# A two-layer hybrid encoder on one core: gate wait, entry roundings, additions to x, root spread and low halves reordered

## The reference

```python
def _layer(x, pos, l, ...):
    h = _rms(x, attn_norm[l])
    z = h @ w_in[l]                       # dq, dk, dv, c_q, c_kv, k_pe
    dq, dk = _rope(...), _rope(...)       # 4 heads x 2 maps of 64
    y_diff = _diff_attention(dq, dk, dv, lam, diff_subln[l], lam_init)
    qh = _rms(c_q, q_a_norm[l]) @ w_q_b[l]
    kvh = _rms(c_kv, kv_a_norm[l]) @ w_kv_b[l]
    y_mla = _mla_attention(q_nope, q_pe, k_nope, k_pe, v)     # 4 heads
    x = x + concat([y_diff, y_mla]) @ w_o[l]
    h = _rms(x, ffn_norm[l])
    return x + (silu(h @ w_gate[l]) * (h @ w_up[l])) @ w_down[l]   # 2816 wide

y = _rms(_layer(_layer(x, 0), 1), final_norm)
```

## Time and profile before

| | |
|---|---|
| Median of 3 runs | 2415.0 us (2414.55 to 2415.11) |
| The profiled execution | 2414.82 us, of it the span 2413.0 us |
| TensorE busy | 2355.6 us (98%) |
| VectorE busy | 1748.3 us (72%) |
| GpSimd busy | 847.4 us (35%) |
| ScalarE busy | 769.1 us (32%) |
| Mean granted TensorE clock | 0.992 of full speed |

### The profile page before, as it was taken

How to read it: one execution, slowest core, us unless ns; L and a number is a source line. 1 busy time by engine, 2 the same in 40 slices (tenths; PEclk the granted TensorE clock), 3 DMA queues, 4 the chain that set the end, 5 groups by cost and what they waited for, 6 DMA issues and landing times.

```text
span 2413.0 us, 32364 instructions
## 1 busy us (share of the span) xinstructions
PE 2355.6 (98%) x11064; PEld 1950.9 (81%) x11064; DVE 1748.3 (72%) x3031; ACT 769.1 (32%) x1492; POOL 847.4 (35%) x640
## 2 busy tenths in 40 slices
PE   8999999999999999999999999999999999999997
PEld 6877888878888888888788788878788888888875
DVE  7997388777677777766758965898666666666676
ACT  5555145532222222222224532454222222222212
POOL 4313000176666666663200010003544444444422
PEclk9999999999999999999999999999999999999998
DMA  8624541344333333331332235223211111111122
GB/s 302 218 79 147 198 162 53 113 174 134 130 125 127 130 130 120 116 120 59 108 140 106 83 126 208 91 88 131 88 53 52 52 52 52 52 52 52 44 78 79
DMA packets 55105, 266.92 MB, mean 111 GB/s; under 512 B 6496, under 2 KB 6624, under 8 KB 36960
## 3 DMA queue, kind: packets, MB, share of 16 engines
q1 hardware_dynamic: 54288, 264.83, 31.7%
q10 hardware_dynamic: 720, 0.86, 0.1%
HBM read 196.45 MB, written 69.21 MB: 110 GB/s over the span
## 4 chain that ended last, share of the span: by engine, by line
PE 79%; DVE 9%; issue 4%; ACT 2%; POOL 2%; DMA 0%; DVEq 0%; ACTq 0%; POOLq 0%; SPq 0%
PE bank L480 25%; PE bank L482 25%; PE bank L481 24%; PE bank L990 2%; DVE x L1830 2%; PE bank L828 1%; DVE u_lo L1816 1%; DVE silu L1805 1%; POOL w L690 1%; PE bank L836 1%; POOL acc L711 1%; DVE aT_lo L1776 0%; DVE qpe L1651 0%; DMA raw<-in_wffn 0%; POOL w L685 0%
## 5 line engine op out<-in xcount | busy, mean ns | idle before, releaser
L480 PE MATMUL bank<-h_hi,w 128*128 128x512 f32 x1792 | 703.6, 393 | 6.1 <-issue 6.1
L482 PE MATMUL bank<-h_hi,w 128*128 128x512 f32 x1792 | 699.5, 390 | 0.0
L481 PE MATMUL bank<-h_lo,w 128*128 128x512 f32 x1792 | 699.0, 390 | 0.0
L1830 DVE TENSOR_TENSOR x<-x,bank 128x512 f32<-128x512 f32 x768 | 470.7, 682 | 4.2 <-PE bank L482 1.2
L690 POOL TENSOR_TENSOR w<-raw,w 128x512 fp32r<-128x512 f32 x230 | 333.1, 1472 | 268.7 <-ACT w L1364 118.6
L480 PEld LDWEIGHTS bank<-h_hi,w 128*128 128x128 f32 x1792 | 337.6, 188 | 75.7 <-issue 6.9
L482 PEld LDWEIGHTS bank<-h_hi,w 128*128 128x128 f32 x1792 | 337.3, 188 | 71.0
L481 PEld LDWEIGHTS bank<-h_lo,w 128*128 128x128 f32 x1792 | 337.7, 188 | 69.1
L742 POOL TENSOR_TENSOR wd<-down_raw,wd 128x512 fp32r<-128x512 f32 x120 | 162.9, 1366 | 485.0 <-ACT wd L1441 485.0
L480 PE MATMUL bank<-u_hi,wd 128*128 128x512 f32 x560 | 220.9, 394 | 9.8 <-DVE x L1830 4.7
L481 PE MATMUL bank<-u_lo,wd 128*128 128x512 f32 x560 | 218.8, 391 | 0.0
(11 more groups left out here) (213 smaller groups left out, 3967.4 us busy)
## 6 DMA issues: line engine op xcount, KB each, us to landing
w<-parked SPq DMA_DIRECT2D x81, 1024.0 KB, 4.8
raw<-in_wffn SPq DMA_DIRECT2D x88, 512.0 KB, 3.6
parked<-w SPq DMA_DIRECT2D x27, 1024.0 KB, 6.5
parked<-p SPq DMA_DIRECT2D x27, 1024.0 KB, 4.8
down_raw<-in_wffn SPq DMA_DIRECT2D x44, 512.0 KB, 3.6
raw<-in_watt SPq DMA_DIRECT2D x27, 512.0 KB, 4.5
praw<-in_watt SPq DMA_DIRECT2D x27, 512.0 KB, 5.7
x_kept<-x SPq DMA_DIRECT2D x4, 2048.0 KB, 9.4
```

The costliest lines, as they stand in the source:

```text
L480: nc.tensor.matmul(out_ap, lhs[0], rhs[0], start=first, stop=False)
L481: nc.tensor.matmul(out_ap, lhs[0], rhs[1], start=False, stop=False)
L482: return nc.tensor.matmul(out_ap, lhs[1], rhs[0], start=False, stop=last)
L1830: nc.vector.tensor_tensor(xn, xn, bank[banks + m][:], op).then_inc(s_acc.sem, 1)
```

## The change

Six things:
- `TENSOR_ORDER`: `RB y2` goes from behind `P vm1` to behind `P vm2`, in all four halves. (The rest of the table is only wrapped at other places.)
- `GPSIMD_ORDER`: `W 23` goes from between `AD 4` and `AD 5` to behind `AD 7`.
- In the three later halves GpSimd makes the seven low halves of the normed tiles (`later_half`), in the order y0, y1, ckv, cq, cq, y2, y3, then adds the squares. VectorE's `AL` does nothing there.
- At the FFN's entry ScalarE makes the slots' high halves (`entry_hi`), after its squares 3, 5, 6 and 7 (`ENTRY_ROUNDS`), GpSimd only the low halves. The first gate tile waits for x's addition `ob6`, the second for `ob7`.
- In the eleventh step VectorE's additions `previous(SEVEN)` go ahead of `gated_lo(0)`, in both layers.
- At the end batch 0's squares are added by VectorE (`square_add`), `SUMS_BEFORE` is 4, `SPREAD_BEFORE` 1, `POOL_SQUARES` 4; VectorE's outputs and last additions are interleaved otherwise.

```diff
-    W 17 | W 18 | W 19 | AD 0 | AD 1 | AD 2 | W 20 | W 21 | W 22 | AD 3 | AD 4 | W 23 | AD 5 | AD 6 | AD 7 | W 24 |
+    | W 18 | W 19 | AD 0 | AD 1 | AD 2 | W 20 | W 21 | W 22 | AD 3 | AD 4 | AD 5 | AD 6 | AD 7 | W 23 | W 24 | W 25 |
...
+ENTRY_ROUNDS = [3, 5, 6, 7]
...
-POOL_SQUARES = 5
+POOL_SQUARES = 4
-SUMS_BEFORE, SPREAD_BEFORE = 6, 5
+SUMS_BEFORE, SPREAD_BEFORE = 4, 1
...
-            add_squares("tail", 0, 1)
+            def later_half(l, b):
+
+                for name in NORMED:
+                    for q, n in enumerate(NORMED[name]):
+                        pool.wait_ge(s_t_hi.sem, s_t_hi.half_at(l, b, n))
+                        dst, src = normed_target(name, q)
+                        nc.gpsimd.tensor_tensor(dst[1], src, dst[0].bitcast(F32), ALU.subtract).then_inc(s_t_lo.sem, 1)
+                add_squares("tail", l, b)
+
+            later_half(0, 1)
             for l in range(L):
                 if l:
                     for b in range(B):
-                        add_squares("tail", l, b)
+                        later_half(l, b)
                 for j in range(GCH):
                     pool.wait_ge(s_mm.sem, s_mm.half_at(l, 1, CHUNK_FREE[NCH - WS_ATT + j] if j < WS_ATT else NMM - 1))
-                    ffn_split(l, 0, j)
+                    ffn_split(l, 0, j, True)
...
-                add_squares("next", l)
+                if l < L - 1:
+                    add_squares("next", l)
...
-                        pe.wait_ge(s_xo.sem, s_xo.half_at(l, 1, len(OUTS) - 1))
+                        pe.wait_ge(s_xo.sem, s_xo.half_at(l, 1, OUTS["ob7" if ev else "ob6"]))
...
+                def entry_hi(j):
+                    act.wait_ge(s_raw[j % RAW].sem, s_raw[j % RAW].step_at(l, 0, j // RAW))
+                    act.wait_ge(s_mm.sem, s_mm.half_at(l, 1, CHUNK_FREE[NCH - WS_ATT + j] if j < WS_ATT else NMM - 1))
+                    for cols in spans(2):
+                        last = nc.scalar.activation(w[j][0][:, cols], raw[:, j % RAW, cols], ACT.Copy)
+                    last.then_inc(s_hi.sem, 1)
+
                 for k in range(KT):
                     norm_square("last", l, 0, k)
                     x_hi("last", l, 0, k)
+                    if k in ENTRY_ROUNDS:
+                        entry_hi(ENTRY_ROUNDS.index(k))
...
                         elif kind == "AL":
-                            stat_lo(l, b, what)
+                            if l == 0 and b == 0:
+                                stat_lo(l, b, what)
...
                     gated(SEVEN, ev, silu[ev % 2], {1: (1,), 2: (3,)}.get(ev) if final else {3: (3,)}.get(ev), unit[1])
+                    if ev == 0:
+                        previous(SEVEN)
                     gated_lo(ev, unit)
                     if ev == 0:
-                        previous(SEVEN)
                         dve.wait_ge(s_acc.sem, s_acc.step_at(l, SEVEN - 1, NACC - 1))
...
                 for ev in range(KT):
                     down_add(ev)
+                    if final and ev:
+                        square_add("next", l, ev - 1)
+                if final:
+                    square_add("next", l, KT - 1)
...
-            for k in range(4):
-                down_add(KT + k)
             output(0, 6)
             output(0, 7)
-            for k in range(4, KT):
+            for k in range(POOL_SQUARES + 2):
                 down_add(KT + k)
-                if k > POOL_SQUARES:
-                    final_add(k - 1)
-            final_add(KT - 1)
+            final_add(4)
+            down_add(KT + 6)
+            final_add(5)
+            down_add(KT + 7)
+            final_add(6)
+            final_add(7)
```

More of the change, by code:

```diff
@@ L71 @@
 TENSOR_ORDER = order("""
[L72 to L81, removed]
+    V | P q0 | P k0 | P q1 | S 0 | Pa k1 | S 1 | Pb k1 | T 0 | S 2 | Pa q2 | S 3 | T 1 | Pb q2 | Pa k2 | S 4 | T 2 | A
+    0 | S 5 | Pb k2 | T 3 | Pa q3 | A 1 | S 6 | T 4 | Pb q3 | ST y0 | S 7 | T 5 | P k3 | S 8 | T 6 | Pa kpe | A 2 | S
+    9 | Pb kpe | T 7 | RB y0 | Pa ckv | S 10 | A 3 | T 8 | S 11 | Pb ckv | T 9 | ST y1 | S 12 | T 10 | Pa cq0 | RB y1
+    | S 13 | Pa cq1 | ST ckv | T 11 | Pb cq0 | S 14 | RB ckv | Pb cq1 | S 15 | ST cq | A 4 | T 12 | RB cq | T 13 | A 5
+    | T 14 | P kn0 | P pe0 | P qn0 | T 15 | ST y2 | A 6 | A 7 | S 16 | P vm0 | S 17 | P vm1 | P vm2 | RB y2 | S 18 | P
+    vm3 | T 16 | P kn1 | ST y3 | P qn1 | S 19 | P kn2 | RB y3 | S 20 | P pe1 | S 21 | T 17 | S 22 | P qn2 | T 18 | A 8
+    | S 23 | P kn3 | P oa0 | T 19 | P qn3 | T 20 | A 9 | S 24 | S 25 | S 26 | S 27 | T 21 | P oa1 | S 28 | T 22 | P
+    oa2 | T 23 | A 10 | S 29 | T 24 | S 30 | A 11 | T 25 | P oa3 | T 26 | P oa4 | T 27 | S 31 | A 12 | T 28 | A 13 |
+    ST n | T 29 | P oa5 | T 30 | P oa6 | T 31 | A 14 | A 15 | P oa7 | P ob0 | P ob1 | P ob2 | RB n | P ob3 | P ob4 | P
+    ob5 | P ob6 | P ob7
 """)
@@ L110 @@
 GPSIMD_ORDER = order("""
-    W 0 | W 1 | W 2 | W 3 | W 4 | W 5 | W 6 | W 7 | W 8 | W 9 | W 10 | W 11 | W 12 | W 13 | W 14 | W 15 | W 16 |
-    W 17 | W 18 | W 19 | AD 0 | AD 1 | AD 2 | W 20 | W 21 | W 22 | AD 3 | AD 4 | W 23 | AD 5 | AD 6 | AD 7 | W 24 |
-    W 25 | W 26
+    W 0 | W 1 | W 2 | W 3 | W 4 | W 5 | W 6 | W 7 | W 8 | W 9 | W 10 | W 11 | W 12 | W 13 | W 14 | W 15 | W 16 | W 17
+    | W 18 | W 19 | AD 0 | AD 1 | AD 2 | W 20 | W 21 | W 22 | AD 3 | AD 4 | AD 5 | AD 6 | AD 7 | W 23 | W 24 | W 25 |
+    W 26
 """)
@@ L675, in _ @@
             pool.memset(ones[:], 1.0).then_inc(s_pre, 1)
-            for c in (s_lo, s_add, s_a_sum, s_a_lo):
+            for c in (s_lo, s_add, s_a_sum, s_a_lo, s_t_lo):
                 pool.sem_inc(c.sem, SEED)
@@ L1528, in _ @@
             for c in (s_plain_lo, s_rope_read, s_roped, s_rope_lo, s_xo, s_max, s_prob, s_at_lo, s_ym_lo, s_dg, s_t,
-                      s_t_lo, s_x_lo, s_gate, s_up, s_gated, s_u_lo, s_xf, s_link, s_t_sum, s_acc,
+                      s_x_lo, s_gate, s_up, s_gated, s_u_lo, s_xf, s_link, s_t_sum, s_acc,
                       s_back):
@@ L1955, in _ @@
             nc.vector.tensor_tensor(zg[:], zg[:], row, ALU.mult).then_inc(s_gate.sem, 1)
+            dve.wait_ge(s_pe, 2)
+            output(0, 0)
             dve.wait_ge(s_silu.sem, s_silu.step_at(l, SEVEN, 3))
             nc.vector.tensor_tensor(silu[1][:], silu[1][:], row, ALU.mult).then_inc(s_up.sem, 1)
-            dve.wait_ge(s_pe, 2)
-            for m in range(3):
+            for m in range(1, 5):
                 output(0, m)
@@ L1963, in _ @@
             nc.vector.tensor_tensor(silu[1][:], zu[:], silu[1][:], ALU.mult).then_inc(s_gated.sem, 1)
-            output(0, 3)
+            output(0, 5)
             gated_lo(3, LAST_UNITS[3])
-            output(0, 4)
-            output(0, 5)
-            for k in range(4):
-                down_add(KT + k)
             output(0, 6)
             output(0, 7)
-            for k in range(4, KT):
+            for k in range(POOL_SQUARES + 2):
                 down_add(KT + k)
-                if k > POOL_SQUARES:
-                    final_add(k - 1)
-            final_add(KT - 1)
+            final_add(4)
[4 more added lines that the diff above has]
+            final_add(7)
             rsqrt_column(final, D, bank[0][:, 0:NT], (s_pe, 3), s_final)
```

## The result

The changed kernel takes 2402.4 us (median of 5 runs, 2401.7 to 2403.9), the kernel before 2415.0 us (5 runs beside them, 2413.0 to 2416.0): a ratio of 0.9950, 95% interval 0.9936 to 0.9965. 2403.2 us had been forecast. The profiled execution took 2402.24 us with a span of 2400.4 us, 12.6 us less than the span before.

The account below looks back on a forecast made before the run. TensorE, busy 2355.6 of 2413.0 us, was taken as the bound, so only its idle time and lower-clock stretches could move. Gains less losses made 11.8 us: 2415.0 - 11.8 = 2403.2 us, own range 2400.5 to 2406, whole range 2398.5 to 2409.5.

Parts of the forecast that it names:

- layer 0's first half: W 23 behind AD 7 shortens the 1.88 us wait before the sums, gain 1.7 us; with RB y2's loss, +1.4 us.
- cq: Three later halves: GpSimd's cq low halves make tile pe0 begin later, a loss of 1.5 us a half, 4.5 in all.
- the low halves buy nothing: Three later halves: taking 21 subtractions, 14.3 us, off VectorE gains nothing by itself.
- RB y2: Spread behind P vm2, four halves: vm2 still waits for vm0's low half, a loss of 0.3 us each, 1.2 us.
- Entry, layer 0: FFN entry: first gate tile starts sooner, but a new 2.6 us wait comes at the spread; gain 3.2 us.
- Entry, layer 1: FFN entry: the gain is the whole stall before the first gate tile, 3.1 us.
- both last steps: Layers' last steps: additions first free a bank sooner, gain 3.4 us in layer 0 and 2.0 in layer 1.
- The end: Kernel's end: no wait before the sums at k = 4, slow stretch gone, last wait 3.0 us; gain 4.4 us.
- Rival A: Clock falls behind the new waits (cq's, layer 0's before the spread): one fall 2406.6 us, two 2410.0; chance 0.25.
- Rival D: Better: slow stretch in 224 to 232 goes, cq costs 0.8 us a half: 2398.5 us; chance 0.15.

Follow-up runs that it names:

- experiment 10: Changed kernel with low halves back on VectorE, RB y2 ahead of P vm2, GpSimd held behind layer 0's entry root, last sums one k later: 2392.6 us.

## Why the prediction was right, and where it was not

- **The sum was right, 2403.2 against 2402.4, because errors cancelled**: too little at the entry (1.9 us) and in layer 0's first half (0.5), too much for cq (2.2), a missed wait (3.4).
- **Missed: RB y3.** The prediction said that the low halves buy nothing, since "the roots' chains begin with TensorE's own sums", and that "only cq's two and y3's are needed soon". It asked which consumer of a moved tile would be late, and not which chain on VectorE the moved instruction would stand beside. And the first of these two statements is wrong for root y3: its first link, `ms<-ls`, stands in the kernel ahead of the wait for the sums, and starts as soon as VectorE has made kn1's low half. ScalarE makes kn1's high half and then y2's. The one releases kn1's low half on VectorE, with the link behind it; the other releases GpSimd. So the two meet: GpSimd begins at 415.11, 1356.07 and 1595.90, the link at 415.15, 1356.11 and 1595.95. That 0.04 us, and not any dependence, gives GpSimd the first place in all three halves; what the opposite order would cost was not tested. The row for the price stood in the earlier trace rows, and I had priced it as busy time only. The Trainium skill says in "SBUF — State Buffer", section "SBUF: two separate sides", that the pair of ports is locked for a whole instruction by whichever of the two starts first, on VectorE's side by an operation in a mode with two ports or with two inputs in SBUF. The 1.27 us beside 1.29 us agree, and so does the condition: the link reads `ls` as both of its inputs, while operations with an input in PSUM are not held (last section).
- **cq: mechanism right, size wrong.** 1.5 us a half were forecast, 0.78 measured. The forecast let GpSimd wait 0.5 us for VectorE's combining of probabilities. It was the other way round: GpSimd's two operations ran back to back in 2.50 us, VectorE's small link beside them took 1.06 us and its combination 1.72. The wait before pe0 is 1.01 us.

```profile
1334.40 1.14 ACT L1362 ACTIVATE cq_hi<-cq_t 128x512 fp32r<-128x512 f32 x2
...
1335.10 2.50 POOL L791 TENSOR_TENSOR cq_lo<-cq_t,cq_hi 128x512 fp32r<-128x512 f32 x2 [8.15 <-ACT cq_hi L1362]
1335.33 1.06 DVE L1747 SCALAR_TENSOR_TENSOR rc<-ls,lamv,rc 128x1 f32<-128x1 f32 x1
...
1336.43 1.72 DVE L1750 SCALAR_TENSOR_TENSOR e<-e,rc,e 128x512 f32<-128x512 f32 x1
...
1337.71 0.47 PE L482 MATMUL bank<-cq_hi,w 128*128 128x512 f32 x1 [1.01 <-issue]
```

- **RB y2: right.** 0.3 us forecast with ends 0 and 0.65, 0.45 measured: v_lo moved by nothing, and the spread came on top.
- **Entry, layer 0: right in kind.** The stall and the slow stretch went, and the new wait at the spread came, 0.69 us instead of 2.6. The root has thirteen links here, one more than the forecast counted. GpSimd began on the raw tile at 515.81, when it had landed, and not at 513.7; eight links of the root had passed freely by then, and four were held instead of seven.
- **Entry, layer 1, and both last steps: right** within 0.3 us each.
- **The end: 1.0 us too much.** TensorE reached k = 4 when forecast, but VectorE's last addition of squares came 1.1 us later: with additions of squares between them, the additions to x take 1.2 us a piece, so that the last x was made 1.2 us later, against the matmuls, than in the earlier trace rows, which the forecast had taken over unchanged. One k later (experiment 10) the wait is gone.
- **Rival A was half right**: the clock fell behind none of the new waits, but behind an old one (187), for 1.6 us. **Rival D** was right on both its parts: the slow stretch of 224 to 231 went, and cq cost 0.8 us. It had been given 0.15; without RB y3's 3.4 us the result would have been 2399.0, near its 2398.5.
